# First token block taken from x tiles scaled ahead of their transposes, the first up weights rounded on GpSimd, and x's fifth tile squared on ScalarE

## The reference

```
def rmsnorm(x, g):
    r = rsqrt(mean(x * x, axis=-1) + EPS)
    return x * r * g

def swiglu(x, w_gate, w_up, w_down):
    return (silu(x @ w_gate) * (x @ w_up)) @ w_down

h = x + 0.5 * swiglu(rmsnorm(x, ffn1_norm), ffn1_w_gate, ffn1_w_up, ffn1_w_down)
p = rmsnorm(h, mix_norm) @ w_in            # split into the two mixer groups
h = h + concat(s_out, c_out) @ w_out
h = h + 0.5 * swiglu(rmsnorm(h, ffn2_norm), ffn2_w_gate, ffn2_w_up, ffn2_w_down)
```

## Time and profile before

| | |
|---|---|
| runs, median (lowest to highest) | 1778.51 us (1778.49 to 1779.38) |
| the profiled execution's own time | 1777.77 us |
| its span from first to last instruction | 1775.8 us |
| PE busy | 1761.2 us, 99% |
| DVE, ACT, POOL busy | 1318.1, 650.6, 642.7 us |
| mean granted clock of PE | 0.998 of full speed |
| chain that ended last | 97% PE, 2% DVE |

### The profile page before, as it was taken

How to read it: one execution, slowest core, us unless ns; L and a number is a source line. 1 busy time by engine, 2 the same in 40 slices (tenths; PEclk the granted TensorE clock), 3 DMA queues, 4 the chain that set the end, 5 groups by cost and what they waited for, 6 DMA issues and landing times.

```text
span 1775.8 us, 31747 instructions
## 1 busy us (share of the span) xinstructions
PE 1761.2 (99%) x11953; PEld 1749.0 (98%) x11953; DVE 1318.1 (74%) x2434; ACT 650.6 (37%) x1278; POOL 642.7 (36%) x669
## 2 busy tenths in 40 slices
PE   8999999999999999999999999999999999999998
PEld 7999999999999999999999999999999999999998
DVE  7658978778877876813775769977887797788766
ACT  7411333333433333533112545333333333333324
POOL 2787232332333232203995221233233322323321
PEclk9999999999999999999999999999999999999999
DMA  6142111112111111365113501111111111111112
GB/s 174 36 131 94 45 54 49 54 48 61 42 54 54 48 54 51 136 131 124 48 42 115 169 14 54 48 54 48 54 48 54 54 46 57 48 54 48 54 49 96
DMA packets 162663, 119.75 MB, mean 67 GB/s; under 512 B 10274, under 2 KB 156258, under 8 KB 162004
## 3 DMA queue, kind: packets, MB, share of 16 engines
q1 hardware_dynamic: 157028, 110.10, 21.1%
q0 software_dynamic: 864, 5.28, 0.9%
q10 hardware_dynamic: 4624, 2.36, 0.6%
HBM read 102.01 MB, written 15.72 MB: 66 GB/s over the span
## 4 chain that ended last, share of the span: by engine, by line
PE 97%; DVE 2%; ACT 0%; issue 0%; DVEq 0%; POOL 0%; POOLq 0%
PE bank_pair L1142 26%; PE bank_pair L1144 25%; PE bank_pair L1143 25%; PE bank_down L1142 6%; PE bank_down L1144 6%; PE bank_down L1143 6%; DVE HT L2324 1%; DVE XL L2347 1%; PE bank_pair L1559 0%; PE bank_pair L1531 0%; PE bank_pair L1655 0%; PE bank_pair L1550 0%; PE bank_pair L1252 0%; PE bank_down L1294 0%; DVE T L2341 0%; DVE S L2341 0%
## 5 line engine op out<-in xcount | busy, mean ns | idle before, releaser
L1142 PE MATMUL bank_pair<-XHM,U_hi 128*128 128x344 f32 x720 | 230.4, 320 | 0.2 <-DVE XLM L2369 0.2
L1144 PE MATMUL bank_pair<-XHM,U_lo 128*128 128x344 f32 x720 | 229.7, 319 | 0.0
L1143 PE MATMUL bank_pair<-XLM,U_hi 128*128 128x344 f32 x720 | 229.7, 319 | 0.0
L2587 DVE SCALAR_TENSOR_TENSOR HT<-bank_pair,HT 128x344 f32<-128x344 f32 x378 | 186.2, 508 | 50.9 <-PE bank_pair L1144 50.7
L3244 POOL TENSOR_TENSOR U_lo<-AST,U_hi 128x512 fp32r<-128x512 f32 x74 | 106.0, 1434 | 266.2 <-ACT U_hi L1719 266.2
L1142 PE MATMUL bank_pair<-XH,U_hi 128*128 128x344 f32 x608 | 194.1, 319 | 0.0
L1144 PE MATMUL bank_pair<-XH,U_lo 128*128 128x344 f32 x608 | 194.1, 319 | 0.0
L1143 PE MATMUL bank_pair<-XL,U_hi 128*128 128x344 f32 x608 | 194.0, 319 | 0.0
L1142 PE MATMUL bank_pair<-XH,WH 128*128 128x344 f32 x576 | 186.6, 324 | 4.4 <-DVE XL L2347 4.3
L1143 PE MATMUL bank_pair<-XL,WH 128*128 128x344 f32 x576 | 184.2, 320 | 0.0
L1144 PE MATMUL bank_pair<-XH,WL 128*128 128x344 f32 x576 | 184.2, 320 | 0.0
(11 more groups left out here) (402 smaller groups left out, 4920.9 us busy)
## 6 DMA issues: line engine op xcount, KB each, us to landing
DQ_raw<-in_ffn_w_down SPq DMA_DIRECT2D x52, 256.0 KB, 2.9
U_raw<-in_ffn_w_gate SPq DMA_DIRECT2D x40, 256.0 KB, 3.0
AST<-in_ffn_w_gate SPq DMA_DIRECT2D x40, 256.0 KB, 3.0
U_raw<-in_ffn_w_up SPq DMA_DIRECT2D x40, 256.0 KB, 3.3
AST<-in_ffn_w_up SPq DMA_DIRECT2D x40, 256.0 KB, 2.9
RAW<-in_w_in SPq DMA_DIRECT2D x16, 512.0 KB, 4.1
DQR<-in_ffn_w_down SPq DMA_DIRECT2D x25, 256.0 KB, 2.9
X<-in_x_prompt SPq DMA_DIRECT2D x8, 512.0 KB, 8.4
```

The lines of the kernel that those rows point to most:

```text
L1142: pe.matmul(out, wh, xh, start=first, stop=False, skip_group_check=onto)
L1143: pe.matmul(out, wh, xl, start=False, stop=False, skip_group_check=onto)
L1144: return pe.matmul(out, wl, xh, start=False, stop=last, skip_group_check=onto)
L2587: dve.scalar_tensor_tensor(ht, STEP_BANKS[STEP_BANK[n]][:, 0:TW], 0.5, ht, ALU.mult, ALU.add).then_inc(pair_free, 1)
```

## The change

- Each of x's tiles 0 to 2 is multiplied by its factor on DVE as it lies, tokens on partitions (`x_scale`), into `HR` and `X2S`. PE then transposes chunk c of all three into one PSUM bank, 128 + 128 + 88 columns (`x_chunk`). ACT rounds the bank with the gain as a scale into `XH`, and DVE takes bank * gain - XH into `XL` in one instruction (`first_block`). The pass over `HT` and `R` for block 0 is gone; `HT` and `R` of tiles 0 to 2 are still made, later.
- The tables of PE's, ACT's and DVE's order are written anew for the start.
- The first up weights are rounded by GpSimd, ahead of its small parameter loads.
- Tile 4 is squared by ACT, not by DVE (`BY_VECTOR`).
- The group j = 1 near 965 us waits for `T0` and `CB` on one semaphore ahead of both products.

```diff
-BY_VECTOR = (4, 7)
+BY_VECTOR = (7,)
...
+        scaled_tile = [HR[:, 0, 0:D], HR[:, 1, 0:D], X2S[:, :]]
+        x_pieces = ((0, 0, P), (1, P, P), (2, 2 * P, TW - 2 * P))
+        def chunk_bank(c):
+            return AB[0][1 + c % 2][:, 0:TW]
...
-                             CAD[:, 8 * j:8 * j + 8, C16:]).then_inc(y_state[j] if j < 2 else y_tab[j], 16)
+                             CAD[:, 8 * j:8 * j + 8, C16:]).then_inc(y_tab[j], 16)
...
+            def x_chunk(c):
+                pe.wait_ge(x_scaled, 3)
+                if c >= 2:
+                    pe.wait_ge(*low_count(0, c - 2))
+                for s, at, n in x_pieces:
+                    out, src = chunk_bank(c)[:, at:at + n], scaled_tile[s][:, c * P:(c + 1) * P]
+                    if n == P:
+                        pe.transpose(out, src, IDENT[:, :])
+                    else:
+                        pe.matmul(out, src, IDENT[:, 0:n], start=True, stop=True).then_inc(xn_tmp, 1)
...
-            x_next((0, 1), (0,))
-            x_next((2,), (1, 2))
-            ffn("1", DOWN1, 0, {(0, 0, 0): lambda: x_next((3,), ()), (0, 0, 2): lambda: x_next((4,), ()),
+            x_next((0, 1), ())
+            x_chunk(0)
+            x_chunk(1)
+            ffn("1", DOWN1, 0, {(0, 0, 0): lambda: x_behind(2, (), ()), (0, 0, 1): lambda: x_behind(3, (), (0, 1, 2)),
...
-                pe.wait_ge(y_tab[j], 16 if j < 2 else 32)
+                pe.wait_ge(y_tab[j], 16 if j == 0 else 32)
...
+                    if i < DC:
+                        act.wait_ge(xn_tmp, i + 1)
+                        act.activation(XH[:, i, cols(0)], chunk_bank(i), ACT.Copy, scale=GAIN[:, 0, i:i + 1]).then_inc(xn_hi, 1)
...
+            def x_scale(s):
+                dve.wait_ge(x_in[s], 16)
+                dve.wait_ge(rcp_x, s + 1)
+                dve.tensor_scalar(scaled_tile[s], X[:, s, :], RS[:, s:s + 1], None, ALU.mult).then_inc(x_scaled, 1)
+            def first_block(after):
+                dve.wait_ge(gain_in, 16)
+                for c in range(DC):
+                    if c in after:
+                        after[c]()
+                    dve.wait_ge(xn_hi, c + 1)
+                    dve.scalar_tensor_tensor(XL[:, c, cols(0)], chunk_bank(c), GAIN[:, 0, c:c + 1], f(XH[:, c, cols(0)]),
+                                             ALU.mult, ALU.subtract).then_inc(xn_low, 1)
...
-            x_scaled(0, 2, {1: lambda: first_lo(0), 3: lambda: (x_root(3), first_lo(1)), 4: lambda: x_square(4), 5: lambda: split_lo(1, 0), 6: lambda: x_root(4),
-                            7: lambda: x_root(5)})
+            first_block({0: lambda: first_lo(0), 1: lambda: x_copies(1), 2: lambda: first_lo(1), 5: lambda: x_copies(2),
+                         6: lambda: x_root(3), 7: lambda: split_lo(1, 0)})
...
+            pool.wait_ge(raw_full[1], 16)
+            pool.tensor_copy(WH[:, 1, :], RAW[:, 1, :]).then_inc(w_hi[1], 1)
```

More of the change, by code:

```diff
@@ L490, in hybrid_trunk @@
         st2 = ExitStack()
+        sb("over_XHL", [P, 2 * DC - 1, NT], F32, st2)
+        X2S = sb("X2S", [P, D], F32, st2)
+        st2.close()
+        st2 = ExitStack()
         sb("over_XHM", [P, 6, 4, TW], F32, st2)
@@ L677, in hybrid_trunk @@
         y_tab = [sem(f"y_tab_{j}") for j in range(WC)]
-        y_state = [sem(f"y_state_{j}") for j in range(2)]
+        y_state = [sem("y_state_0")]
+        x_scaled = sem("x_scaled")
         z_out = [sem(f"z_out_{j}") for j in range(WC)]
@@ L1306, in x_spread, with x_behind @@
                           ).then_inc(spread_full, 1)
+            def x_chunk(c):
[8 more added lines that the diff above has]
+                        pe.matmul(out, src, IDENT[:, 0:n], start=True, stop=True).then_inc(xn_tmp, 1)
+            def x_behind(chunk, transposes, spreads):
+                if chunk is not None:
+                    x_chunk(chunk)
+                x_next(transposes, spreads)
             def x_next(transposes, spreads):
@@ L1891, in _ @@
             x_rms(2)
+            act.wait_ge(gain_in, 16)
+            first_up(0)
+            uppers(0, 2)
+            first_up(1)
+            uppers(2, 4)
             x_spread(0)
@@ L2491, in _, with x_copies @@
             dve.wait_ge(const_done, 3)
-            def x_tile(s):
+            def x_copies(s):
                 m = P if s < S8 else DEC
                 for h in range(2):
-                    if h == 1 and s == 2:
-                        x_root(s)
                     dve.wait_ge(xt_full, 2 * s + h + 1)
@@ L2527, in x_scaled @@
                 normalised(0, tb, after)
[L2529 to L2535 removed]
+            x_copies(0)
+            x_root(0)
+            x_scale(0)
+            x_root(1)
+            x_scale(1)
+            x_root(2)
+            x_scale(2)
+            first_block({0: lambda: first_lo(0), 1: lambda: x_copies(1), 2: lambda: first_lo(1), 5: lambda: x_copies(2),
+                         6: lambda: x_root(3), 7: lambda: split_lo(1, 0)})
+            x_root(4)
+            x_root(5)
+            normalise_block(1, 5, {9: lambda: x_square(7), 10: lambda: x_root(6), 12: lambda: x_tile(7), 14: lambda: x_tile(8)})
+            normalise_block(2, 8)
             lambda_rows()
```

42 lines of the change are left out of this document (17 added, 25 removed).

## The result

The changed kernel takes 1785.94 us, the median of six runs (1784.16 to 1789.39), against 1778.5 us before (six runs, 1777.92 to 1780.13). The ratio is 1.0043, with a 95% interval of 1.003 to 1.0056: slower by 7.4 us. The forecast was 1785.0 us with a range of 1779.8 to 1788.0, and slower as the likeliest side.

A forecast was written before the change was run, and what follows sets the result against it. TensorE, busy 99% of the span, bounds the kernel. 5.9 us at the start plus 0.6 at 969 us made 6.5 on the profiled 1777.77 us: 1784.3, as a median 1785.0 us, range 1779.8 to 1788.0.

The forecast's parts named there:

- the walk: PE, ACT and DVE queues stepped in program order, before and changed; put PE's leave of the first products at +5.9 us.
- block 1: Second 344-column block of x's 1032 tokens; first scaling forecast at 30.3 us, first product at 34.7 against 29.5.
- tile 7's transposes: Ahead of the last two up products in PE's queue; forecast to wait 2.5 us for ACT, to 32.7 us.
- The waits for the split up weights and for tile 4's copies: Two PE waits forecast at the start: 0.9 us (at 22.7) and 0.7 us (at 25.8).
- the ring: Block 0's loop: a product frees PE for a later chunk, ACT rounds it, DVE takes it off; said to hold ACT.
- some 9 us of bare work after the ring lets go: ACT's squares, copies, four roundings and spreads before factor 5's copy; cited against PE being fed without a gap (0.07).
- the chunk: Work added to PE: two transposes of 128 columns and a product of 88, 0.30 us each, 2.4 us for eight.
- three scalings: DVE's scaling of x's tiles 0 to 2 at the start, taken at 0.95 us each, between 0.68 and 1.22.
- the 0.68 end: Low price in us for one DVE tile scaling, from one of two copies; would make the sum 0.6 smaller.
- second stretch: Slow-clock rival at the start: another 3.4 us at 1.2 GHz, costing 1.4 at block 0 and 0.5 at tile 7; chance 0.14.
- The ceiling: Best case at the start: PE ends at 42.5, 3.9 us below 46.41; the slow clock takes back about 1.7.
- The second place: At 969 us, PE waits for group 1's CB ahead of the T0 products: +0.6 us, 0 to 1.0.

The follow-up runs named there:

- the kernel with the tables apart: The changed kernel with group 1's CB again on a semaphore of its own, waited for behind the T0 products: 1785.41 us, ratio 1.004.
- Early squares: The changed kernel with only ACT's squares of tiles 3, 4 and 5 moved ahead in its order: 1787.69 us, ratio 1.0052.
- the slots changed: The changed kernel with the same work in new slots on PE, ACT and DVE: 1781.15 us, ratio 1.0014.
- Done alone: The kernel before with only group 1's T0 and CB joined on one semaphore: 1778.70 us, ratio 1.0003.
- the changed kernel with the clock kept: The changed kernel in its own order with unread identity transposes (20, 6 and 21) in three of PE's waits: 1783.86 us, ratio 1.0028.
- the kernel with the edit: The changed kernel with earlier slots, filler transposes, group 0's tables joined instead of group 1's, and each 88-token piece made by a transpose: 1778.70 us, ratio 0.9998.

## Why the prediction was right, and where its reasons were not

**The size at the start.** +5.9 us by the walk, +5.89 measured (46.41 to 52.30). Single steps: ACT's square of tile 5 near 26 (26.05), its copy of factor 5 near 30 (30.14), block 1's first scaling at 30.3 (30.45), tile 7's transposes to 32.7 (32.78), block 1's first product 34.7 (34.86). The waits for the split up weights and for tile 4's copies are 0.62 and 0.47 us (0.9 and 0.7 forecast), tile 7's 2.22 (2.5). That the sum agrees to the hundredth is luck: the kernel with the tables apart has the same orders at the start and leaves at 53.78, and the terms below are off both ways.

**The cause given for it was half wrong.** The prediction says that ACT is held by the ring, does its squares late, and that the late factor 5 comes from "some 9 us of bare work after the ring lets go". The walk had PE's table in it, so its times were right; the sentence drawn from it named the wrong queue. Early squares gained nothing, and turned into ACT waits for PE's spreads. PE's table put spread 5 behind the fifth up product and tile 7's transposes one product further, while ACT's copy of tile 6, for which these wait, stands behind a rounding of block 1 that needs factor 5. With the slots changed, the same work on ACT has factor 5 ready 4.5 us earlier and the kernel gains 4.8 us. The price belongs to the order, not to the load. That it is PE's order more than ACT's or DVE's is what the brackets say and the edit of ACT's order alone supports; no run changed PE's alone.

**A term that was mis-sized: the chunk.** The forecast took 0.30 us for each. In the timeline above the chunk takes 0.36 (18.70 to 19.06), 0.41 ahead of transposes (19.61 to 20.02), and the product behind it occupies 0.55 (19.06 to 19.61) where products in a row take 0.47. The excess lies in the first of its three rows, 0.24 (19.06 to 19.30) for some 0.16, and a product behind a tile's transposes has it too (18.14 to 18.39), so it isn't the chunks' alone. With it a chunk comes to some 0.45, and all eight to at most 3.6 us instead of 2.4, by estimate. The piece of 88 columns was counted by its share of columns; written as a product with the identity it is listed with two operations for one. Against that stand three scalings of 0.75 us, where 0.95 was taken, nearer to the low end that came from the copy. The Trainium skill's page "VectorE: DVE Perf Modes", section "Mode 2×_2P — use both read ports for one tensor", has an fp32 operation with one tensor inside SBUF pass two elements a cycle, and the prediction read the 0.68 end from that; the trace's 0.75 agrees to within 0.07 us. The first product came at 11.68 instead of 12.2, and PE's three waits were 0.8 us shorter together than forecast. These errors worked against each other.

**The clock.** The forecast kept 3.4 us of slow clock at the start for both kernels and gave its second stretch as a rival: +1.9 us, at 0.14. The profiled execution has no second stretch at the start; the kernels with the tables apart and with the squares early have it, just behind tile 7's wait, and leave at 53.78 and 54.12. In the runs, the transposes that keep the clock give 2.1 us. So this rival was true as well, in some executions. The ceiling charged 1.7 us for a slow stretch like that of the kernel before; in that kernel itself the stretch cost nothing (46.42 against 46.41).

**The second place.** +0.6 us forecast, with 0 to 1.0. Done alone it measured 0.3 us, undone 0.5 us. The profiled execution lost 3.64 us there, by a wait of 1.94 and a slow stretch behind it that the forecast didn't think of. The step of the forecast was right where CB took the 4.3 us of its row: 0.43 to 0.56 us of wait in three profiles. What it had too small is the spread of that landing time, 5.4 to 5.8 us in three others. It also left out that the third group can wait for its own tables, 0.30 to 0.62 us in four profiles with the second group's semaphores apart.

**GpSimd's rounding.** It took 1.87 us in the changed kernel and 1.04 in eight others, inside the bounds of 0 to 2.37, and PE never waited for it. "Hidden" was true for the changed kernel, which has slack on DVE, but the walk had no line for what it does to DVE: up to 0.8 us on one instruction.

**The sum of the runs.** Of 7.4 us, 2.1 went with the transposes that keep the clock, by way of the slow stretches and perhaps of CB's load. Of the 5.3 left, that kernel's profile puts about 5 on the order and the chunks (it leaves at 51.76, 5.35 later than before) and some 0.6 on the tables (8.74 us from the first to the third group, against 8.10). The forecast's 6.5 was made of 5.9 and 0.6: 1.2 us more than the 5.3, and nothing for what the clock adds, 2.1. The two errors offset each other in part, and the forecast came within 0.9 us of 7.4 by some luck.

## What to carry to other kernels

When an engine's result comes late, read what ended the idle time just before it before blaming its load: an engine that idles 1.47 us ahead of the late instruction isn't short of time there, and the first place to look is the order of whoever it waits for. Idle time on TensorE can have a second price behind it, the slow clock, and filling it is worth trying where TensorE is the bound: the same filler transposes gave 1.9 and 2.1 us in two kernels and nothing in the two whose first block waits for VectorE. A semaphore saved by joining two waits is cheapest where both loads land long before their use; a load that lands in 4.3 us in one profile can take 5.8 in the next.

## What the runs showed of the hardware

- **The clock behind idle time.** After idle stretches of 1.9 to 2.4 us on PE, the clock was at 1.2 GHz for 3.4 us in some executions and 5.6 to 6.8 in others of nearly the same start, and not at all from 10 to 20 us in the five kernels with the stretch filled by 20 or 22 transposes of 128 columns. Behind the same 2.22 us at tile 7 it fell in two profiles and stayed up in one.
- **GpSimd and VectorE held each other up.** GpSimd's rounding of 128x1024 takes 1.04 us when it starts first (13.29 against 13.35, or 13.37 against 13.45), and then the VectorE instruction with two SBUF inputs beside it takes 1.35 instead of 0.57, or in the changed kernel with the clock kept, 1.77 instead of 0.95 (first row below). In the changed kernel's own profile it was the other way round: GpSimd's took 1.87 and VectorE's 0.95 was unchanged (last two rows). Their starts are listed only 0.02 us apart, so which was first can't be read there. The held instruction ends a fixed time behind the other's end: VectorE's scaling 0.37 us in three kernels, its low half of 768 columns 0.81 us in three. So one waits for the other as a whole. The Trainium skill's page "SBUF — State Buffer", section "Who interferes with whom", describes it: with two SBUF inputs on the one side and an SBUF read on the other, the later one is blocked until the first has finished. The traces agree, by the 0.37 and the 0.81 us above.

```profile
13.45 1.77 DVE L2555 TENSOR_TENSOR WL<-RAW,WH 128x768 fp32r<-128x768 f32 x1
```

```profile
13.11 1.87 POOL L3146 CAST WH<-RAW 128x1024 fp32r<-128x1024 f32 x1 [2.86 <-DMA RAW<-in_ffn_w_up]
...
13.13 0.95 DVE L2553 TENSOR_TENSOR WL<-RAW,WH 128x768 fp32r<-128x768 f32 x1
```

- **A transpose of 88 tokens is cheaper than the product with the identity.** From the start of the chunk to the tile transposes behind it, it took 0.30 us (19.23 to 19.53) with the piece as a transpose, against 0.41 in the changed kernel (19.61 to 20.02). The rows of the kernel with the edit:

```profile
19.23 0.38 PE L1326 MATMUL bank_pair<-IDENT,HR 128*128 128x128 f32 x2
19.45 0.24 PE L1326 MATMUL bank_pair<-IDENT,X2S 88*128 88x88 f32 x1
19.53 1.04 PE L1306 MATMUL bank_down<-IDENT,X 128*128 128x128 f32 x8
```
